# The triangular inverse of a gated delta rule: 32x32 blocks in place of 64x64 ones in its first four levels

## The reference, cut to what matters

```python
A = jnp.where(strict, jnp.einsum('bhncd,bhnjd->bhncj', kb, k) * decay, 0.0)
eye = jnp.eye(chunk, dtype=A.dtype)
rhs = jnp.concatenate([v * beta[..., None], kb * jnp.exp(gam)[..., None]], axis=-1)
sol = lax.linalg.triangular_solve(eye + A, rhs, left_side=True, lower=True, unit_diagonal=True)
```

## Time and profile before

| | |
|---|---|
| median of 3 runs | 1453.37 us |
| runs | 1453.24, 1461.93, 1453.37 us |
| profiled execution | 1465.4 us, span 1463.6 us |
| TensorE matmul | 1291.1 us busy, 88% of the span |
| VectorE, ScalarE, GpSimd | 42%, 26%, 14% |
| mean granted TensorE clock | 0.933 |
| mixing loop | 8 tiles, about 385 to 823 us of the span |
| the matmuls of line 1431 | 2560 passes, 103.7 us busy |

### The profile page before, as it was taken

The page is one execution under the profiler, slowest core; times in us unless marked ns, Lnnn a source line. Parts: engine busy times, 40 slices in busy tenths (PEclk is TensorE's granted clock), DMA queues, the critical chain, the costliest instruction groups (busy, mean ns, idle before and its releaser), DMA issues. The chain is left out here.

```text
span 1463.6 us, 21846 instructions
## 1 busy us (share of the span) xinstructions
PE 1291.1 (88%) x8380; PEld 890.4 (61%) x8380; DVE 616.3 (42%) x1130; ACT 375.8 (26%) x735; POOL 209.9 (14%) x275
## 2 busy tenths in 40 slices
PE   6999999953898898898998948899999999974987
PEld 4669999942566576676676625344454444533876
DVE  2324554127746557657558226111112111116564
ACT  2322323111334243343443212111111111113332
POOL 0000000002212212312212001022222222110110
PEclk9999999975899799999999879999999999996999
DMA  6211233147121120220220129599999999945451
GB/s 203 88 51 58 86 101 100 45 72 234 46 64 41 50 76 14 90 75 14 90 71 4 43 87 345 194 324 337 344 336 361 347 349 340 341 178 216 145 174 45
DMA packets 151335, 226.08 MB, mean 154 GB/s; under 512 B 12651, under 2 KB 123835, under 8 KB 146670
## 3 DMA queue, kind: packets, MB, share of 16 engines
q1 hardware_dynamic: 130606, 171.27, 35.4%
q10 hardware_dynamic: 11184, 28.48, 5.4%
q0 software_dynamic: 9504, 25.77, 4.5%
HBM read 183.37 MB, written 46.76 MB: 157 GB/s over the span
## 5 line engine op out<-in xcount | busy, mean ns | idle before, releaser
L1658 PE MATMUL psum<-experts 128*128 128x512 f32 x528 | 232.2, 592 | 2.6 <-DVE experts L1680 2.6
L627 PE MATMUL psum<-split_parts 128*128 128x344 f32 x1224 | 194.1, 321 | 0.0
L627 PEld LDWEIGHTS psum<-split_parts 128*128 128x128 f32 x1224 | 193.9, 188 | 0.1
L1658 PEld LDWEIGHTS psum<-experts 128*128 128x128 f32 x528 | 100.2, 190 | 128.3 <-issue 125.3
L1431 PE MATMUL psum<-decode_and_mix 64*64 64x64 f32 x2560 | 103.7, 234 | 36.8 <-DVE decode_and_mix L1166 29.3
L1431 PEld LDWEIGHTS psum<-decode_and_mix 64*64 64x64 f32 x2560 | 92.7, 146 | 64.1 <-issue 62.9
L1695 DVE COPY experts<-psum 128x256 f32<-128x256 f32 x33 | 14.0, 425 | 274.7 <-PE psum L1665 274.7
L1405 PE MATMUL psum<-decode_and_mix 128*128 128x512 f32 x256 | 121.1, 618 | 0.7 <-ACT decode_and_mix L1288 0.7
L1674 PE MATMUL psum<-experts 128*128 128x512 f32 x264 | 119.2, 594 | 1.5 <-ACTq L1711 1.0
L2261 PE MATMUL psum<-last_parts 128*128 128x512 f32 x432 | 102.3, 397 | 0.0
L2261 PEld LDWEIGHTS psum<-last_parts 128*128 128x128 f32 x432 | 82.2, 192 | 17.0
(11 more groups left out here) (369 smaller groups left out, 1716.4 us busy)
## 6 DMA issues: line engine op xcount, KB each, us to landing
experts<-in_w_gate SPq DMA_DIRECT2D x33, 1024.0 KB, 7.0
experts<-in_w_up SPq DMA_DIRECT2D x33, 1024.0 KB, 11.5
experts<-in_w_down SPq DMA_DIRECT2D x33, 1024.0 KB, 13.3
project<-in_w_in SPq DMA_DIRECT2D x18, 512.0 KB, 4.9
last<-ye_d SPq DMA_DIRECT2D x16, 512.0 KB, 7.3
conv_out_d<-project ACTq DMA_DIRECT2D x12, 512.0 KB, 3.0
decode_and_mix<-conv_out_d SPq DMA_DIRECT2D x8, 768.0 KB, 7.6
until_mixed<-in_x_prompt SPq DMA_DIRECT2D x8, 512.0 KB
```

Of the source, the lines that this page charges most:

```text
L627: mm = nc.tensor.matmul(thirds(u)[:, b], w[:, u, k, :], x[:, k, b * TB:(b + 1) * TB], start=(i == 0 and k == 0), stop=(i == 2 and k == KD ...
L1658: mm = nc.tensor.matmul(bank(2 + s.v), xgT[s.v][:, k, :], wgu[s.u][:, k, :], start=(k == 0), stop=(k == KD - 1))
```

## The change

A function `blocks` is added, and levels 1 to 4 call it in place of `quarters`; level 5 keeps `quarters`. For each head it multiplies the four 32x32 blocks on the diagonal of the 128 partitions (two in each chunk) and writes only those blocks of the bank; the rest of the bank keeps what it held. A group becomes 16 matmuls, 32 passes, of 32 rows and 32 columns by 32 moving columns, in four different places of the array in turn. Everything that is copied afterwards keeps its size.

```diff
+                def blocks(g, out, left, right):
+                    settle(pe)
+                    for s in range(4 * g, 4 * g + 4):
+                        for b in range(4):
+                            rows, own = slice(32 * b, 32 * b + 32), slice(32 * (b % 2), 32 * (b % 2) + 32)
+                            at = (s % 4) * HD + own.start
+                            mm = T.matmul(bank(out + g)[rows, at:at + 32], left[rows, s, own], right[rows, s, own], start=True, stop=True)
+                    return mm
+
                 def level(t, l):
                     for g in range(2):
                         pe.wait_ge(S(f"T{g}"), LV * t + l)
-                        quarters(g, 0, ATd, T_).then_inc(S(f"X{g}_ps"), 1)
+                        (blocks if l < LV else quarters)(g, 0, ATd, T_).then_inc(S(f"X{g}_ps"), 1)
                     for g in range(2):
                         pe.wait_ge(S(f"X{g}"), LV * t + l)
-                        quarters(g, 6, Xs, MT).then_inc(S(f"PT{g}_ps"), 1)
+                        (blocks if l < LV else quarters)(g, 6, Xs, MT).then_inc(S(f"PT{g}_ps"), 1)
```

## The result

The changed kernel took 1543.32 us (median of 4 runs, 1540.17 to 1551.87) against 1457.03 us for the kernel before (4 runs). The ratio is 1.0592, 95% interval 1.0553 to 1.0631. The profiled execution has a span of 1542.7 us, 79.1 us more than before. The forecast was 1444 us, with a range of 1437 to 1475.

The account below looks back on a forecast made before the run. TensorE was busy 88%, but waits handed round three engines bound most levels. Looped tiles 6.7 us, first tile 1.5 and half-clock tiles 1.5 made 9.7, taken as 9: 1453.4 - 9 = 1444 us, range 1437 to 1475.

Parts of the forecast that it names:

- The price of a pass: Changed products: 31 ns a pass in one place, four places side by side, -0.19 us a group.
- The floor rival: Every changed group: a minimum time per pass makes it slower, 1473 us at 22 ns, 1493 at 29; chance 0.18.
- two at a time: Changed groups: only two array places run together, +0.03 us a group, 1450 to 1458 us; chance 0.20.
- The path: Loop tile: one group of level 2, two each of levels 3 and 4 set its length; 0.95 us a tile.
- the groups taken as hidden: Loop tile: groups outside the five counted, such as two of level 4 beside copies, save nothing.
- level 1 gives up to 0.5 us in a tile with the longer half clock: Three of seven loop tiles: level 1's last three groups run at half clock, 0.5 us each tile, 1.5 us together.
- The queue can feed it: TensorE's queue: sends a pass per 12 ns, 0.4 us for 32, so a group can't exceed 0.47 us.
- The clock rival: Levels 2 and 3: idler TensorE gets longer or more half-clock stretches, 3 to 10 us, 1447 to 1454 us; chance 0.06.

Follow-up runs that it names:

- Five groups: Kernel before, with 32x32 blocks only in PT of group 0 (level 2), X and PT of group 1 (level 3), X of group 0, PT of group 1 (level 4): 1454.88 us.
- Levels 3 and 4: Kernel before, with 32x32 blocks in all groups of these two levels only, 64x64 elsewhere: 1460.21 us, ratio 1.0011.
- level 4 alone: Kernel before, with 32x32 blocks in this level only, 64x64 elsewhere: 1458.99 us, ratio 1.0052.
- levels 3 and 4 with PT of level 2: Kernel before, with 32x32 blocks in these two levels and in PT of both groups of level 2: 1463.28 us, ratio 1.0045.
- the last kernel: Kernel before, with blocks in five groups of the looped tiles and in all groups of levels 1 to 4 of the first tile: 1450.36 us, ratio 0.9938.
- with the branch gone or covered: Changed kernel, with TensorE's looped tiles written out (1482.39 us), or with six large unread matmuls before the branch (1521.87 us).

## Why the prediction was wrong

- **The price of a pass: right.** Four places run side by side. A group saves 0.23 us in the row, 0.45 for 0.68; the forecast took 0.19 from bounds of -0.22 and +0.52. The floor rival is out (32 passes with their end in 0.45 us, 14 ns a pass at most), and so is two at a time. The rule of the Trainium skill, "TensorE: Matmul & The Clock Gate", section "Wait — 56ns, not 53.3ns?", of some 25 ns between starts does not hold over the whole array here.
- **The path: right in the main.** Five groups were to give 0.95 us a tile; they gave 0.9. Levels 3 and 4 gave 1.0, level 4 alone 0.6 where two groups promised 0.4, and levels 3 and 4 with PT of level 2 gave 1.2, so the groups taken as hidden are worth up to 0.3 us together. That level 1 gives up to 0.5 us in a tile with the longer half clock is borne out (up to 0.6); that it gives nothing in the others could not be seen. In the total, these gains show only in the last kernel (0.9938).
- **"The queue can feed it": this step failed.** I asked how fast the queue sends out instructions that it has, 12 ns a pass, and not where they come from when a round has 512 more. The doubled code was costed at nothing with no cover named. In a tile that is hit, it costs a stall of 4.6 us at the loop's end and 7.0 us by the half clock behind it, 14 us with the late code and the clock further on; five of six jumps back were hit, and the branch accounts for some 60 of the 86 us. No rival held it, so a range up to 1475 us could not.
- **The clock rival** had the right instrument and the wrong size: at most one stretch more a tile, 3 to 10 us in all, where the mean granted clock fell from 0.933 to 0.882. The largest part came from idle time in the branch, which it did not name. Idle time in the levels may still hold a part: with the branch gone or covered, the kernels with all blocks kept 13.7 to 20.5 us at half clock a tile.

What stays open: why the step comes between 1,580 and 1,644 instructions, when a round of 1,772 ran once without a transfer in its trace; what keeps the clock down in the levels when all four have blocks; and the tile of about 62 us that most profiles with a fitting loop have.

## What to carry to other kernels

Whoever multiplies the instructions in a hardware loop should count them per round first, and look at the instruction queue on the page: a loop that fetches nothing today can begin to fetch everything, and it does so in one step. Put the small products only where they are on the path, and in code that runs once. When a branch takes microseconds, price the clock behind it too: here 4.6 us of idle time cost another 7.0, since TensorE restarted at half clock.

## What the hardware showed unexpectedly

- Float32 products of 32x32 in four places of the array on the diagonal run four abreast: 32 passes in 0.45 us with their end.
- A loop of 1,580 TensorE instructions is not fetched again; one of 1,644 is, in five of six jumps back, with nine transfers a round (`q8 instruction: 9, 0.15, 1.1%` over 545 to 612 us of that profile), with a branch of 5.8 us (median) in place of 0.2.
- Straight-line code of 1,247 instructions in a tile of 56 us costs nothing that could be measured (0.9999); the kernel with 1,759 a tile was 2.2% slower, in part by code that came late.
- Nine transfers a round bring more than the round: one holds 256 instructions, and the round has 1,644 or 1,772.
- Five microseconds of work that is queued ahead of the branch keeps the clock up through the stall, and a kernel with more work in it became 21 us faster.
